# Where TensorE's operands begin in SBUF: 192 bytes behind a multiple of 2048 bytes in place of on one

## What is computed

```python
def first_block(x, ...):
    for layer in range(2):
        h = rms_norm(x, mix_norm[layer])
        if layer == 0: x = x + gdn_shortconv_mixer(h, ...)   # gated delta rule + short convolution
        else:          x = x + nsa_mixer(h, ...)             # compressed, selected and windowed attention
        h = rms_norm(x, mlp_norm[layer])
        x = x + jnp.square(jax.nn.relu(h @ w_up[layer])) @ w_down[layer]      # 1024 -> 4096 -> 1024
    return rms_norm(x, final_norm)

def second_block(x, ...):
    for l in range(2):
        p = _rms_norm(x, norm_g[l]) @ w_in[l]
        # latent attention with 8 heads, and a 2-D Fourier branch
        y_a = (attention(...) * silu(z_a)) @ w_attn_proj[l]
        y_f = (jnp.real(jnp.fft.fft2(u_f, norm='ortho')) * silu(z_f)) @ w_fourier_proj[l]
        x = x + (sigmoid(g_a + b[0]) * y_a + sigmoid(g_f + b[1]) * y_f) @ w_out[l]
    return x
```

## The kernel before

| tensor | offset before | modulo 2048 |
|---|---|---|
| common | 17056 | 672 |
| x | 18432 | 0 |
| raw, w_hi, w_lo | 34816, 47104, 59392 | 0 |
| h_hi, h_lo, a_hi, a_lo | 161792, 178176, 194560, 210944 | 0 |
| t_hi, t_lo | 116736, 133120 | 0 |
| w_hi_s, w_lo_s | 100288, 108480 | 1984 |
| phase0, phase1, phase2 | 92416 | 256 |
| kc | 137216 | 0 |

## Time and profile before

### The profile page before, as it was taken

One profiled execution on the slowest core, in us unless ns is written; L12 is line 12 of the kernel. 1 busy time (PEld: TensorE's weight loads), 2 busy tenths in 40 slices (PEclk: granted clock), 3 DMA queues, 4 the chain that ended last, 5 costly groups with the idle time before them and its releaser, 6 DMA issues.

```text
span 2057.1 us, 29944 instructions
## 1 busy us (share of the span) xinstructions
PE 2035.6 (99%) x12084; PEld 1665.0 (81%) x12084; DVE 1195.0 (58%) x1977; ACT 1000.1 (49%) x1623; POOL 728.6 (35%) x316
## 2 busy tenths in 40 slices
PE   8999999999999999999999999999999999999999
PEld 5777778989888886668889898778788887878887
DVE  7885566665647156775666655657734354774331
ACT  7752464444436326773644443656742344765321
POOL 3332143444444631004434344344034443402443
PEclk9999999999999999999999999999999999999999
DMA  4432123322332430002333322222022222201222
GB/s 158 134 128 71 47 96 103 101 100 98 103 103 86 148 95 32 1 2 96 103 103 103 101 95 98 86 93 82 12 81 94 93 100 89 87 22 62 93 94 90
DMA packets 62727, 179.17 MB, mean 87 GB/s; under 512 B 17776, under 2 KB 18160, under 8 KB 62592
## 3 DMA queue, kind: packets, MB, share of 16 engines
q1 hardware_dynamic: 47600, 168.04, 24.1%
q10 hardware_dynamic: 14992, 9.22, 1.6%
HBM read 171.97 MB, written 3.70 MB: 85 GB/s over the span
## 4 chain that ended last, share of the span: by engine, by line
PE 95%; DVE 2%; ACT 2%; issue 0%; DMA 0%; POOL 0%; SPq 0%; DVEq 0%; ACTq 0%
PE banks L842 22%; PE banks L844 21%; PE banks L843 21%; PE banks L948 4%; PE banks L947 4%; PE banks L946 4%; PE banks L1297 2%; PE banks L1331 2%; PE banks L1310 2%; PE banks L1420 1%; PE banks L1433 1%; PE banks L1405 1%; PE banks L893 1%; DVE norm L2282 1%; PE banks L1411 1%; PE banks L1015 1%
## 5 line engine op out<-in xcount | busy, mean ns | idle before, releaser
L3050 POOL TENSOR_TENSOR w_lo<-raw,w_hi 128x1024 fp32r<-128x1024 f32 (+2 forms) x312 | 728.4, 2336 | 1312.1 <-ACT w_hi L1558 1312.0
L1558 ACT ACTIVATE w_hi<-raw 128x1024 fp32r<-128x1024 f32 (+2 forms) x312 | 317.4, 1018 | 489.8 <-PE banks L844 337.4
L842 PE MATMUL banks<-h_lo,w_hi 128*128 128x512 f32 (+1 forms) x992 | 400.4, 404 | 10.4 <-POOL w_lo L3050 8.6
L844 PE MATMUL banks<-h_hi,w_hi 128*128 128x512 f32 (+1 forms) x992 | 387.6, 391 | 0.0
L843 PE MATMUL banks<-h_hi,w_lo 128*128 128x512 f32 (+1 forms) x992 | 387.4, 390 | 0.0
L842 PE MATMUL banks<-a_lo,w_hi 128*128 128x512 f32 x768 | 304.1, 396 | 0.0
L843 PE MATMUL banks<-a_hi,w_lo 128*128 128x512 f32 x768 | 299.4, 390 | 0.0
L844 PE MATMUL banks<-a_hi,w_hi 128*128 128x512 f32 x768 | 299.1, 389 | 0.0
L842 PEld LDWEIGHTS banks<-h_lo,w_hi 128*128 128x128 f32 (+1 forms) x992 | 185.9, 187 | 57.8 <-issue 9.3
L2303 DVE TENSOR_TENSOR x<-x,banks 128x512 f32<-128x512 f32 x168 | 114.9, 684 | 182.8 <-PE banks L844 182.7
L843 PEld LDWEIGHTS banks<-h_hi,w_lo 128*128 128x128 f32 (+1 forms) x992 | 186.0, 188 | 41.6 <-issue 5.0
(11 more groups left out here) (413 smaller groups left out, 3708.4 us busy)
## 6 DMA issues: line engine op xcount, KB each, us to landing
raw<-in_weights SPq DMA_DIRECT2D x311, 512.0 KB, 3.2
x<-in_x SPq DMA_DIRECT2D x4, 512.0 KB, 5.8
AT<-row_dram ACTq DMA_DIRECT2D x4, 512.0 KB, 7.7
out<-x SPq DMA_DIRECT2D x8, 256.0 KB, 2.0
eg<-row_dram ACTq DMA_DIRECT2D x8, 128.0 KB, 3.0
phase<-in_phase ACTq DMA_DIRECT2D x1, 706.0 KB, 5.8
phase<-in_phase ACTq DMA_DIRECT2D x1, 704.0 KB, 4.2
ld_dram<-Ld ACTq DMA_DIRECT2D x1, 512.0 KB, 4.5
```

The costliest lines, as they stand in the source:

```text
L842: mm(out, w_hi, x_lo, start=first, stop=False)
L844: return mm(out, w_hi, x_hi, start=False, stop=last)
L1558: f(c.w_hi[:, b % RING, to], c.raw[:, b % RING, cols], ACT.Copy).then_inc(c.w_hi_ready, 1)
L3050: return nc.gpsimd.tensor_tensor(c.w_lo[:, slot, to], c.raw[:, slot, first:end], c.w_hi[:, slot, to].bitcast(F32), ALU.subtract)
```

## The change

Two lines of `place` are changed:

```diff
     def aligned(n):
-        return (n + 2048 - 1) // 2048 * 2048
+        return (n - 192 + 2048 - 1) // 2048 * 2048 + 192
 ...
-    tail = (top - 2 * 32768) // 2048 * 2048
+    tail = (top - 2 * 32768 - 192) // 2048 * 2048 + 192
```

## The result

| | before | after |
|---|---|---|
| median of 15 runs each | 2057.94 us (2057.27 to 2063.83) | 2062.67 us (2061.62 to 2068.77) |
| ratio, 95% interval | | 1.0026 [1.0018, 1.0033] |
| the profiled execution, its span | 2058.95, 2057.1 us | 2062.72, 2060.9 us |
| ScalarE's copy `ld_dram<-Ld` lands after | 4.5 us | 5.3 us |
| its copy back `Ls<-ld_dram` lands after | 3.2 us | 5.5 us |

The change makes the kernel slower by 4.7 us, 0.26%, and the interval lies on the slow side of no change. The forecast was 2057.7 us and no change: the time lies inside the range given, the sign was not foreseen.

What follows compares the result with a forecast made beforehand. TensorE's matmul time from start to start was taken to bound the kernel. All terms summed to 0 on the profiled 2058.95 us, 1.22 us above the median, so 2057.7 us; 8-in-10 range 2049 to 2066.

Steps and rivals of the forecast that it cites:

- parts 1 to 4: Operand distances, lines touched, crossings of 2048 multiples, weight-tile place: each taken as 0; pace stays 226.7 and 117.7 ns.
- the rival of a crossing cost: Moving operands now crossing a multiple of 2048 bytes cost 1 ns or more: 7.0 us, 2064.7 us; chance 0.2.
- Part 1's reason: Operands of TensorE and other engines move by the same 192 bytes, so distances between streams stay; taken as 0.
- the place decides the meeting of weights and stream: TensorE: absolute places below 512 bytes affect weight loads beside matmuls; a ns less is 8.2 us, 2049.5; chance 0.23.
- part 5: DMA and other engines: `raw` landings fit even at twice the length, ScalarE, VectorE and GpSimd wait for TensorE; taken as 0.
- Everything else that it touches (DMA landings, reads and writes of the other three engines) has cover: Opening: matmul time from start to start is the only lever; work outside it is covered.
- an unchanged pace with a longer span, seen as idle time of PE before L842 released by POOL: Sign of being wrong in another way: TensorE idles before that matmul line, waiting for GpSimd.
- The chance of 0.01: Chance given to a loss elsewhere, outside the matmul pace; a loss of about 1 us counted as no change.
- The range of 2049 to 2066: Whole kernel, in us, for 8 in 10; reaches to the 1 ns ends of the crossing and place rivals.

Runs made afterwards that it cites:

- Experiment 1: Changed kernel with a shift of 256 bytes in place of 192; 2059.08 us against 2058.27, ratio 1.0001.
- Experiment 4: Changed kernel with everything shifted by 64 bytes in place of 192; 2061.65 us against 2058.27, ratio 1.0012.
- 10: Kernel before with PAIR_SHIFT 0 in place of 16, so the weights of `seven` lie on multiples of 512 bytes; one run, 2062.52 us against 2057.78.
- experiment 11: Kernel before with all weights 64 bytes ahead of a multiple of 512, moving operands left in place; 2063.83 us against 2058.03, ratio 1.0033.
- 12: Kernel before with PAIR_SHIFT 32 in place of 16, weights of `seven` 128 bytes ahead of a multiple of 512; 2064.09 us against 2059.14, ratio 1.0022.
- 2: Changed kernel with `Ld` alone put back onto a multiple of 256 (192 + 64); 2059.26 us against 2058.27, ratio 1.0002.
- 3: Kernel before with `Ld` alone moved 64 bytes further on; 2062.56 us against 2058.27, ratio 1.0016.
- 5: Changed kernel with weight block 18 held back until `Ls` has landed; 2058.7 us against 2058.27, ratio 1.0003.
- 6: Kernel before with `Ls` sent only when weight block 18 has landed; 2063.99 us against 2058.27, ratio 1.0026.
- 7: Kernel before with `Ld` alone 32 bytes further on; one run, 2062.82 us.
- experiment 8: Kernel before with `Ld` alone 96 bytes further on; one run, 2067.55 us.
- 9: Kernel before with `Ld` alone 128 bytes further on; one run, 2059.11 us.

## Why the prediction was wrong

- **The pace of the matmuls (parts 1 to 4)** held. 226.7 and 117.7 ns are what they were, L843 has 389 ns, and L1209 lies between 234 and 252 ns. No crossing cost, of which 1 ns each would have been 7.0 us; the rival of a crossing cost is out. Experiment 1 is the cleaner test, since its loss elsewhere is gone: its operands cross the same multiples of 2048, at 1.0001.
- **Part 1's reason** (distances are kept, and if anything costs it is distance) is borne out by experiments 4 and 10 to 12. Experiment 4 moves weights and moving operands by the same 64 bytes and leaves `seven` at 117.7 ns; where 10 to 12 change the distance between the two, the matmuls concerned take about 2 ns more. The rival "the place decides the meeting of weights and stream" named the right two partners and the wrong variable: absolute places moved by 192 bytes did nothing, and the distance was not part of this change.
- **The step that failed is part 5, with "I take 0"**, and with it the sentence of the opening, "Everything else that it touches (DMA landings, reads and writes of the other three engines) has cover". Cover was shown there for `raw` (in flight three blocks deep) and for nothing else. The two copies on ScalarE's queue have none: the first goes in pieces of 128 bytes, the second waits for the first, and VectorE waited for the second 2.0 us in the trace of before. The term put at 0 was 4.6 us: 2.9 of PE's wait and 1.7 at the lower clock.
- **The views that would have shown it** were at hand: the waits of the stretch from 95 to 126 us, with VectorE behind `Ls`; the issues by size, with 4096 packets of 128 bytes; and the two queues, 0.41 us apart. I priced DMA by its largest user, and by size. The page of the Trainium skill quoted above was there to be asked what an address does to a DMA; I asked the skill only what it does to an engine.
- **What would show it wrong**: "an unchanged pace with a longer span, seen as idle time of PE before L842 released by POOL" was half right. The pace is unchanged and PE is idle, but before L893 and released by ScalarE's `sq`. The weights were never late.
- **The chance of 0.01** for a loss elsewhere "of about 1 us" was too small on both counts. The range of 2049 to 2066 held the time, but for a reason (1 ns a crossing) that was not the cause.

## What to carry to other kernels

When a change moves tensors, list every transfer that touches them and ask of each small-piece one what its new address does: here pieces of 128 bytes wanted a start at a multiple of 128. A wait on a DMA that stands in the trace already is where a later landing shows at nearly full price, and two queues that send within half a us of each other are an order that a small delay can turn. And find the place of a loss by comparing the starts of the same work in both traces before looking for its cause: here four rows put all of it ahead of 231 us.

## What the runs showed of the hardware that was not expected

- A copy from SBUF of 4096 pieces of 128 bytes lands after 4.5 to 4.7 us if no piece crosses a multiple of 256, and after 5.3 us if every second one does, whether the offset is 32, 64, 96 or 192 (experiments 1 to 9, before and after). Crossings of a multiple of 128 would fit as well.
- `Ls`, 512 KB, sent 0.4 us behind a block of the same size on another queue lands after 5.1 to 5.6 us (after, 3, 4, 7, 8). It lands after 3.2 us when it is sent 0.41 us ahead, after 3.4, 3.9 and 3.6 when 0.30, 0.26 and 0.18 us ahead (9, 1, 2), and after 3.3 alone (5, 6).
- A wait of 2.5 to 3.6 us of PE was followed by a stretch at 1.2 GHz in each of the profiles that had one at 118 us; one of 0 to 0.8 us at the same place was not. Similar stretches stood elsewhere in single profiles: at 203 us in experiment 8, behind a wait of 1.8 us, and at 786 us before, behind short waits of 0.55, 0.75 and 0.39 us that the trace after has too, without a fall. What decides in such cases is open.
- From start to start, 256-column matmuls of fp32r take 119.9, 117.8 and 120.05 ns with weights 0, 64 and 128 bytes ahead of a multiple of 512 and moving operands on one, and 512-column ones 226.7 and 229.0 ns at 0 and 64. With weights on a multiple of 512 and moving operands 64 bytes behind one (experiment 4), `seven` took 117.7 ns: the distance counts, and not the place. At the same distances `seven` took 117.8 in some stretches and 113.3 in others in experiment 11. Why is open; 113.3 throughout would be worth 2184 x 4.4 ns = 9.6 us.
